# First block of a two-block network: weights converted ahead of the softmax, the memory tokens' squares moved, norms and mixing by heads

## The reference

```python
h = rmsnorm(x, attn_norm_g)                       # x: 512 x 1024
proj = h @ w_in                                   # cut into gla q, k, v, r, low rank; moba q, k, v; mem q
o_gla = gla_chunked(q, k, v, g_log)               # 4 heads, chunks of 64 tokens
o_gla = rmsnorm(o_gla, gla_out_norm_g) * silu(gla_r)
o_moba = softmax attention of 4 heads, causal, with ALiBi, normed q and k
mem_h = rmsnorm(mem, mem_norm_g)                  # mem: 256 x 1024
o_mem = softmax attention of 4 heads into 256 memory tokens, normed q and k
x = x + concat(o_gla, o_moba, o_mem) @ w_out
x = x + hierarchical_moe(rmsnorm(x, ffn_norm_g))  # 32 experts, 2 per token
```

## Time and profile before

| | us |
|---|---|
| median of 3 launches | 1845.45 |
| lowest, highest | 1844.28, 1849.76 |
| the profiled launch, device time | 1845.85 |
| its span, first to last instruction | 1843.4 |
| PE busy in the span | 1723.0 |
| DVE, ACT, POOL busy | 702.5, 603.2, 563.2 |

### The profile page before, as it was taken

How to read it: one execution, slowest core, us unless ns; L and a number is a source line. 1 busy time by engine, 2 the same in 40 slices (tenths; PEclk the granted TensorE clock), 3 DMA queues, 4 the chain that set the end, 5 groups by cost and what they waited for, 6 DMA issues and landing times.

```text
span 1843.4 us, 20373 instructions
## 1 busy us (share of the span) xinstructions
PE 1723.0 (93%) x8350; PEld 1202.3 (65%) x8350; DVE 702.5 (38%) x1058; ACT 603.2 (33%) x786; POOL 563.2 (31%) x263
## 2 busy tenths in 40 slices
PE   8789888799999999988789999999999999999995
PEld 5577655444444443445578987777778788888882
DVE  5544543333433333357851012223344421222335
ACT  5545444111001110124631245554333432322231
POOL 2232224321022201013244434443443444444440
PEclk9889989899999999999999999999999999999997
DMA  5121163499999999961222110111242222222201
GB/s 202 46 69 47 46 248 132 176 419 421 422 421 421 421 421 420 421 254 62 76 91 92 46 47 27 66 46 48 94 178 91 92 92 92 92 92 97 87 35 46
DMA packets 75069, 308.57 MB, mean 167 GB/s; under 512 B 3008, under 2 KB 4448, under 8 KB 50272
## 3 DMA queue, kind: packets, MB, share of 16 engines
q1 hardware_dynamic: 74704, 306.18, 42.5%
q0 software_dynamic: 272, 1.05, 0.2%
HBM read 305.12 MB, written 2.10 MB: 167 GB/s over the span
## 4 chain that ended last, share of the span: by engine, by line
PE 82%; DVE 10%; ACT 4%; issue 2%; POOL 1%; DMA 0%; DVEq 0%; SPq 0%; ACTq 0%
PE ps L846 39%; PE ps L1178 12%; PE ps L888 7%; PE ps L1202 6%; PE ps L1132 4%; PE ps L844 2%; PE ps L1325 2%; PE ps L1147 1%; PE ps L1148 1%; PE ps L1310 1%; ACT sb_slot L1392 1%; PE ps L1346 1%; DVE sb_R L2304 1%; POOL sb_w_parts L786 1%; DVE sb_slot L1797 1%
## 5 line engine op out<-in xcount | busy, mean ns | idle before, releaser
L786 POOL TENSOR_TENSOR sb_w_parts<-sb_slot,sb_w_parts 128x2048 fp32r<-128x2048 f32 x59 | 274.5, 4654 | 411.3 <-ACT sb_w_parts L1392 411.3
L846 PE MATMUL ps<-sb_h_high,sb_w_parts 128*128 128x512 f32 x1120 | 273.3, 396 | 15.5 <-issue 8.2
L846 PEld LDWEIGHTS ps<-sb_h_high,sb_w_parts 128*128 128x128 f32 x1120 | 210.9, 189 | 67.3 <-issue 12.7
L1178 PE MATMUL ps<-sb_slot,sb_hT 128*64 128x512 f32 x768 | 171.1, 594 | 0.0
L1392 ACT ACTIVATE sb_w_parts<-sb_slot 128x2048 fp32r<-128x2048 f32 x59 | 112.7, 1911 | 172.4 <-PE ps L846 172.4
L846 PE MATMUL ps<-sb_hidden_high,sb_w_parts 128*128 128x512 f32 x704 | 165.2, 389 | 1.8 <-ACT sb_hidden_high L1392 1.8
L846 PEld LDWEIGHTS ps<-sb_hidden_high,sb_w_parts 128*128 128x128 f32 x704 | 132.1, 188 | 29.7 <-ACT sb_hidden_high L1392 2.3
L750 POOL TENSOR_TENSOR sb_tile_parts<-sb_slot,sb_tile_parts 128x1024 fp32r<-128x1024 f32 x32 | 76.3, 2387 | 221.5 <-ACT sb_tile_parts L1392 221.5
L846 PE MATMUL ps<-sb_h_low,sb_w_parts 128*128 128x512 f32 x560 | 138.0, 389 | 0.0
L1178 PEld LDWEIGHTS ps<-sb_slot,sb_hT 128*64 128x64 f32 x768 | 53.6, 137 | 106.2 <-issue 106.2
L846 PEld LDWEIGHTS ps<-sb_h_low,sb_w_parts 128*128 128x128 f32 x560 | 105.1, 188 | 21.8
(11 more groups left out here) (312 smaller groups left out, 2675.2 us busy)
## 6 DMA issues: line engine op xcount, KB each, us to landing
sb_slot<-w_up SPq DMA_DIRECT2D x24, 2048.0 KB, 15.5
sb_slot<-w_gate SPq DMA_DIRECT2D x24, 2048.0 KB, 15.4
sb_slot<-w_down SPq DMA_DIRECT2D x21, 2048.0 KB, 16.2
sb_slot<-w_in SPq DMA_DIRECT2D x14, 2048.0 KB, 8.0
sb_R<-w_down SPq DMA_DIRECT2D x11, 2048.0 KB, 15.8
sb_slot<-tiles SPq DMA_DIRECT2D x32, 512.0 KB, 3.4
sb_R<-w_gate SPq DMA_DIRECT2D x8, 2048.0 KB, 15.2
sb_R<-w_up SPq DMA_DIRECT2D x8, 2048.0 KB, 15.8
```

Source lines behind the costliest of these rows:

```text
L786: nc.gpsimd.tensor_tensor(low, raw_part(g), high.bitcast(F32), ALU.subtract).then_inc(w_low, 1)
L846: ins = nc.tensor.matmul(o, w[:, k, at:at + P], h[:, k, :], start=first, stop=last)
L1178: ins = nc.tensor.matmul(ps_[b * CAP:(b + 1) * CAP, bank0, :], xgT[:, k, at:at + CAP], w[:, b, kk * 512:(kk + 1) * 512], start=(k == 0), s ...
```

## The change

The order of the plan is altered, and a few steps are cut in two.

1. A helper split_to(g) puts all conversions up to tile g into the list. In the main loop it is called ahead of soft i for the tile behind the first filling tile, and ahead of silu 3 for out 1. Before, the conversion stood ahead of the tile's job.
2. mem_parts on ACT (8 copies and the squares) moves from the end of pair 0 to the start, ahead of norm 0. Its DVE part is a step of its own, mem_low, behind the low-rank product. The load of mem is issued ahead of tile 3. The squares get a place of their own in R, so that ACT no longer waits for the row sums of x.
3. mem_acc moves up from the end of pair 1 to that of pair 0, mem_sum from pair 2 to the end of pair 1, with the reciprocal in it.
4. The exponentials of the memory pairs free the scores' banks themselves.
5. gla_norm is a step by heads: head 0 of the first half at the end of pair 11, head 1 at the end of pair 12, and around tile r 2 for the second half. intra 1 moves from pair 12 to pair 11, lam from 12 to 14.
6. silu of r 0 and r 1 with mix 0 and 1 move ahead of the evictions of gla_out 1; before, they stood behind tile r 2.
7. One wait is added in the path for overfull experts, which no row of the trace shows running.

```diff
+    def split_to(g):
+        while split[0] <= min(g, len(TILES1) - 1):
+            step("w1", split[0])
+            split[0] += 1
     def tile(name, n):
-        g = TILES1.index((name, n))
-        if g + 1 < len(TILES1):
-            step("w1", g + 1)
+        split_to(TILES1.index((name, n)) + 1)
         job("tile", name, n)
...
-    middle = {2: ["mem_sum"]}
-    late = {0: ["mem_parts"], 1: ["mem_acc"], 2: [("decay", 0)], 4: [("decay", 1)], 5: [("decay_qk", 0)], 8: [("turn_keys", 0), ("intra", 0)],
-            9: [("chunk_state", 0)], 10: [("decay_qk", 1)], 11: [("gla_sum", 0), ("turn_keys", 1)], 12: [("intra", 1), "lam"],
-            13: [("chunk_state", 1)]}
+    late = {0: ["mem_acc"], 1: ["mem_sum"], 2: [("decay", 0)], 4: [("decay", 1)], 5: [("decay_qk", 0)], 8: [("turn_keys", 0), ("intra", 0)],
+            9: [("chunk_state", 0)], 10: [("decay_qk", 1)], 11: [("gla_sum", 0), ("turn_keys", 1), ("intra", 1), ("gla_norm", 0, 0)],
+            12: [("gla_norm", 0, 1)], 13: [("chunk_state", 1)], 14: ["lam"]}
...
     tile("mq", 0)
+    step("mem_parts")
     step("norm", 0)
...
     job("lr")
+    step("mem_low")
     post("mk", 0)
...
         if i < len(PAIRS):
+            if fills[i][0] != "gla_out":
+                split_to(TILES1.index(fills[i][0]) + 1)
             step("soft", i)
...
             step("norm_rows", i)
+            if i == 15:
+                step("silu", 0, 2)
+                step("mix", 0)
+                step("mix", 1)
...
             gla("gla_sum", 1)
-            step("silu", 0, 2)
+            step("gla_norm", 1, 0)
             tile("r", 2)
             step("evict", "r", 2)
-            step("mix", 0)
-            step("mix", 1)
+            step("gla_norm", 1, 1)
     tile("r", 3)
     step("silu", 2, 3)
     step("mix", 2)
+    split_to(TILES1.index(("out", 1)))
     step("evict", "r", 3)
...
+            load(memT, a["memT"].rearrange("(k p) n -> p k n", p=P), ld["mem"])
             tile_load(3)
-            load(memT, a["memT"].rearrange("(k p) n -> p k n", p=P), ld["mem"])
...
-                    act.wait_ge(acc0, 1)
                     fn(memsq, memT, ACT.Square).then_inc(mem_sq, 1)
...
-                            ins = fn(sp[i % 2][:, hh, 0:NM], bank(("score", i, hh))[:, 0:NM], ACT.Exp,
-                                     scale=rq[:, 2 + pr, 2 * qt + hh:2 * qt + hh + 1], **kw)
+                            frees(fn(sp[i % 2][:, hh, 0:NM], bank(("score", i, hh))[:, 0:NM], ACT.Exp,
+                                     scale=rq[:, 2 + pr, 2 * qt + hh:2 * qt + hh + 1], **kw), ("score", i, hh))
...
-                elif kind == "gla_sum":
-                    for hh in range(2):
-                        gla_norm(arg[0], hh)
+                elif kind == "gla_norm":
+                    gla_norm(*arg)
```

More of the change, by code:

```diff
@@ L102, in gla @@
             step(kind, *arg)
-    step("w1", 0)
+    split_to(0)
     step("x_parts")
-    step("w1", 1)
-    job("tile", "mk", 0)
+    tile("mk", 0)
     step("x_squares")
     tile("mq", 0)
+    step("mem_parts")
     step("norm", 0)
@@ L132, in plan @@
             job("values", i - 2)
-        for e in middle.get(i, ()):
-            step(e)
         if i < len(PAIRS):
+            if fills[i][0] != "gla_out":
+                split_to(TILES1.index(fills[i][0]) + 1)
             step("soft", i)
@@ L140, in plan @@
             step("norm_rows", i)
-            if i == 2:
-                step("mem_recip")
+            if i == 15:
+                step("silu", 0, 2)
+                step("mix", 0)
+                step("mix", 1)
             if fills[i][0] == "gla_out":
@@ L353, in build @@
         memT = view(slot[2], 0, KD, NM)
-        memsq = view(R, 6144, KD, NM)
+        memsq = view(R, 9216, KD, NM)
         mem_rstd = view(slot[3], 1664, NM)
@@ L1487, in _ @@
                     act.wait_ge(gla_prod, h + 1)
-                    if h in (0, 2):
+                    if h == 2:
                         finished(act, ("gla_out", 1, 1))
@@ L1579, in _ @@
                         if which == "mem":
-                            ins = fn(sp[i % 2][:, hh, 0:NM], bank(("score", i, hh))[:, 0:NM], ACT.Exp,
-                                     scale=rq[:, 2 + pr, 2 * qt + hh:2 * qt + hh + 1], **kw)
+                            frees(fn(sp[i % 2][:, hh, 0:NM], bank(("score", i, hh))[:, 0:NM], ACT.Exp,
+                                     scale=rq[:, 2 + pr, 2 * qt + hh:2 * qt + hh + 1], **kw), ("score", i, hh))
                         else:
                             w_ = P * (qt + 1)
-                            ins = fn(sp[i % 2][:, hh, 0:w_], sp[i % 2][:, hh, 0:w_], ACT.Exp, **kw)
-                        ins.then_inc(exp_done, 1)
+                            fn(sp[i % 2][:, hh, 0:w_], sp[i % 2][:, hh, 0:w_], ACT.Exp, **kw).then_inc(exp_done, 1)
                 elif kind == "turn":
@@ L1833, in _ @@
                     dve.wait_ge(ld["cst"], 16)
-                elif kind == "mem_parts":
+                elif kind == "mem_low":
                     for k in range(KD):
@@ L1843, in _ @@
                     v.tensor_tensor(mem_rstd, memsq[:, 0, :], memsq[:, 1, :], ALU.add).then_inc(mem_acc, 1)
-                elif kind == "mem_recip":
+                elif kind == "mem_sum":
                     dve.wait_ge(mem_std, 1)
@@ L2030, in _ @@
                     j, w_ = i % 2, NM if which == "mem" else P * (qt + 1)
-                    dve.wait_ge(exp_done, 2 * i + 2)
                     if which == "mem":
                         for hh in range(2):
-                            dve.sem_inc(bank_free[J["score", i, hh] % JB], 1)
+                            taken(dve, ("score", i, hh))
+                    else:
+                        dve.wait_ge(exp_done, 2 * i + 2)
                     link(v.reciprocal(row_inv[:, j, :], row_sum[:, j, :]))
@@ L2257, in over @@
                         choose(o_, CAP, i)
+                        dve.wait_ge(o_["chosen"], i + 1)
                         stepped(v.tensor_scalar(row, row, -float(CAP), None, ALU.add))
```

1 line of the change is left out of this document (added).

## The result

The changed kernel took 1833.08 us in the median of 5 launches (1828.3 to 1833.43), the kernel before 1847.04 in the same comparison (1844.28 to 1851.29): a ratio of 0.9919, with a 95% interval of 0.9903 to 0.9934. Of 1847.04 that is 15.0 us less (12 to 18 by the interval; the medians themselves lie 14.0 apart). Forecast were 15.2 less and 1830. The profiled launch took 1828.52, with a span of 1825.8, 17.6 shorter than the one before. It was one of the quicker launches of the changed kernel: two of the five took about 1828.4, three about 1833.2.

A forecast was written before the change was run, and what follows sets the result against it. The experts were taken as bound by their weight stream, starting with PE, so first-block savings in PE's waits and half clock carry through. 0 + 8.8 + 3.8 + 2.6 = 15.2 off 1845.85 gave 1830; forecast 1823 to 1837, wider range 1816 to 1840.

The forecast's parts named there:

- the start: Start and memory tokens, to 70 us: 5.1 gained and 5.1 lost, so 0; bounds +10 and -3.
- the tail: From gla_out 1 to the output projection: 11.4 won, 8.8 given back, so +2.6; bounds +8 and -3.
- The hold between mem_low and the two POOL passes: In the start: POOL's port lock holds mem_low nearly 4 us; score 0 waits 3.1, about 2 us half clock follow.
- The other half of the step: At mem and pair 1: 3.8 of 7.8 us of waits saved, plus 1.3 of half clock, 5.1 in all.
- Pairs 3 to 7: 88 to 145 us: conversion waits and half clock end, 15.0; later softmaxes give back 6.2; +8.8, bounds 15.0 and 5.
- Pairs 11 to 14: Stop ahead of intra 1 and its half clock go, 5.8; a later bank wait costs 2.0; +3.8, bounds 6.8 and 1.
- the three prices given back: From gla_out 1 on: 2.0 of wait at turn 15, 4.8 ahead of gla_sum 1, 2.0 of half clock; 8.8 together.
- The shift through the experts: Behind the first block: the experts' weight stream starts with PE, so an earlier end moves everything behind by the same amount.
- the rival by which a shorter first block vanishes: Experts: their stream starts with the loads, not with PE, so nothing is gained; 1845 us, chance 0.04.
- the chain: First block: every pair waits for its softmax, pairs 3 to 7 give 5, the rest cancels; 1838 to 1841, chance 0.15.
- The full gain: First block: port and softmax chain do not bite; 28 us at most, 1817 to 1822, chance 0.25.
- The slower one: Tail: silu, mixing and lam ahead of gla_out 1's evictions lose over 15 us against 12.6 won; 1847, chance 0.06.

The follow-up runs named there:

- a1: The changed kernel launched again without any edit, as reference: 1833.59 us, ratio 0.9930 to the kernel before.
- a2: The changed kernel launched a third time without any edit, as reference: 1831.39 us, ratio 0.9926 to the kernel before.
- e4: Changed kernel with mem_low directly behind mem_parts, ahead of the norm of head 0: 1829.58 us, ratio 0.9909 to the kernel before.
- e2: Changed kernel without its early conversions (both added split_to calls taken out): 1839.01 us, ratio 0.9971 to the kernel before.
- e1: The kernel before with only the early conversions put in: 1839.98 us, ratio 0.9968 to the kernel before.
- e10: Changed kernel with the gates' last subtraction one pair later, behind pair 3's softmax: 1825.15 us, ratio 0.9896 to the kernel before.
- e7: Changed kernel with the norms of half 0 and intra 1 in their old places, lam not moved back: 1834.63 us, ratio 0.9934 to the kernel before.
- e5: Changed kernel with lam moved from behind pair 14 to behind norm_rows of pair 10: 1826.68 us, ratio 0.9895 to the kernel before.
- e6: Changed kernel with silu and mix of the first half back behind the second half's norms: 1832.03 us, ratio 0.9911 to the kernel before.
- e9: Changed kernel with mem_low ahead of norm 0, lam behind norm_rows of pair 10, mix 1 behind the evictions of gla_out 1: 1820.72 us, ratio 0.9865.

## Why the prediction was right

The sum was right, 15.2 against 15.0, and so were its kind of terms. That it fits within 0.2 is luck. The repetitions gave 12.9 (a1) and 13.6 (a2), while the profiles up to the router, which is what the terms speak of, gave 18.0, 17.0 and 16.8: there the forecast was 1.6 to 2.8 too low. The rest went behind the router, where the changed kernel had 0.5, 5.9 and 3.0 more than the one profiled launch of the kernel before, by the granted clock. Of the four terms two were too small in the first profile, the start and the tail, one too large and one nearly right.

**The start, 0 forecast, 2.4 measured.** The hold between mem_low and the two POOL passes was there, as the step said. What the step had wrong is its victim. It let DVE stand still for both passes and charged score 0 with a wait of 3.1 and 2 of half clock. In fact POOL stood first, until seven of mem_low's eight subtractions were through, and then DVE, for one pass, and each lost about 2; the keys were ready at 43.57, and PE, which had itself lost 1.8 at tile mk 1 to the stretched passes, came to score 0 only at 45.14. e4 prices the whole collision at 2.0, not 5.1. The other half of the step, 5.1 gained at mem and pair 1, came out as 2.4 + 2.0 = 4.4, with 1.84 at mem_sum and 2.30 at turn 1 left of the 7.8 of waits (4.0 were to stay).

**Pairs 3 to 7, 8.8 forecast, 7.2 measured.** The waits of cv 0 and cv 1 went, and e2 and e1 show that the early conversions did it (82.20 against 75.59; 82.80 to 75.43). The two waits that were to come came with their size: 2.09 at turn 3 (2.0), 2.55 at turn 6 (2.3 to 2.5 more than the old 0.8 were forecast, so less came). Not in the sum were the half clock behind turn 3, 1.7, and two waits at pair 5, 0.98 at its turn and 1.18 ahead of L984; ahead of the first, the gates' subtraction of the second half meets a pass as well (2.72 at 111.01). e10 shows that the hold at turn 3 alone costs 4.1, not 2.0: this was the mis-sized term. One more was too small on the other side. The half clock behind cv 1 was read from 127 to 131 us; from the stop on, in the kernel before, it is

```profile
124.85:131.50 6.65, 6.34 (x26) 0.52 0.39 118
```

and costs 6.34 x 0.48 = 3.0, not 1.9.

**Pairs 11 to 14, 3.8 forecast, 4.3 measured.** intra 1 does not wait, as said. The wait for r 1's bank stayed at 1.04; the rise to 3.0 did not come. On the other side the forecast did not see that the early conversions make this stretch longer: by 4.3 with the old norms and lam's old place (e1), by 57.80 - 56.34 = 1.5 with the new ones (e2). Moving the norms is thus worth 6.65 in the new kernel (e7), not 5.8.

**The tail, 2.6 forecast, 4.1 measured.** 2.52 at turn 15 (2.0), 4.22 at gla_sum 1 (4.8) and 1.5 of clock (2.0): the three prices given back were right within 0.6 each, in all 8.2 for 8.8; 11.4 - 8.2 would be 3.2, and 0.9 more came than these terms say. In a1 and a2, with the same waits and more half clock behind them, the tail gave just the forecast 2.6 (48.62 and 48.60). The cause named for each holds too: lam (e5) and the mixing ahead of the evictions (e6, e9). What the forecast did not see is that both belong to one chain, so that taking lam away also shortens the wait at gla_sum 1.

**The shift through the experts** was one for one, as the reading of the earlier trace rows had it, where the clock allows a comparison: in the five profiles with 37.5 us at half clock behind the router's first matmul, that matmul starts between 239.88 (e9) and 265.61 us (before), and what follows takes 1577.8 to 1578.3. This leaves nothing of the rival by which a shorter first block vanishes. The medians gained 3 to 4 less than the stretches all the same: a1 and a2 had more half clock behind the router (54.6 and 44.4 us) than the profiled launch before (37.5). Whether the earlier start has a part in that no run shows.

Of the rivals, the chain came nearest: after the change PE waits longest for the softmax. But it has 10.7 in six waits over the whole block, 8.1 more than before, and did not take back the whole gain. The full gain, 28, needed the port and the softmax chain to stay quiet; 15.0 came. The slower one would have needed more than 17 at gla_sum 1; 4.2 came, and e6 shows that without edit 6 the time is the same.

Open: e9 and e10 touch different stretches and were not run together. Edit 4 was not taken out by itself, so its share is not known. Why the clock in the unchanged part differs from launch to launch isn't settled; no run here was made for it.

## What to carry to other kernels

Conversions for a tile belong ahead of the softmax that used to precede them, but on a chain of in-order engines this makes later whatever stands behind them: look for the next late step at each place, and put work that nobody needs yet (lam, the last step of the gates, half of the mixing) into a stretch where its engine idles. When two engines collide, ask who waits for each of the two: here PE waited for the one that had not been suspected. A stop of some 2 us can cost nearly double, once as wait and once as a lower clock behind it (2.1 and 1.7 at turn 3); and when a gain is read off, compare stretches up to a common place before medians, since the rest of the launch scatters by more than most of these edits are worth.
